# Weight sums of the Strassen products: made by accumulating DMA instead of VectorE

## The reference

```python
def swiglu(x, w1, w3, w2):
    return (jax.nn.silu(x @ w1) * (x @ w3)) @ w2

h1 = LN1(ALPHA * x + 0.5 * swiglu_1(x))
h2 = LN2(ALPHA * h1 + Mixer(h1))         # pooling, windowed attention, gates
y  = LN3(ALPHA * h2 + 0.5 * swiglu_2(h2))
```

## Time and profile before

| | us |
|---|---|
| median of 3 runs (lowest, highest) | 1071.97 (1071.76, 1073.37) |
| span of the profiled execution | 1069.7 |
| PE busy | 1041.3 |
| DVE busy | 806.8 |
| ACT busy | 480.6 |
| POOL busy | 115.7 |

### The profile page before, as it was taken

How to read it: one execution, slowest core, us unless ns; L and a number is a source line. 1 busy time by engine, 2 the same in 40 slices (tenths; PEclk the granted TensorE clock), 3 DMA queues, 4 the chain that set the end, 5 groups by cost and what they waited for, 6 DMA issues and landing times.

```text
span 1069.7 us, 20766 instructions
## 1 busy us (share of the span) xinstructions
PE 1041.3 (97%) x8177; PEld 1024.2 (96%) x8177; DVE 806.8 (75%) x1310; ACT 480.6 (45%) x849; POOL 115.7 (11%) x123
## 2 busy tenths in 40 slices
PE   8999999999999989999999999989999999999995
PEld 8999999999999979998899999979999999999995
DVE  6994999548996775987555576899589973899766
ACT  5543555215554343474542252645355531455424
POOL 2000000000002455000000015400000000000054
PEclk9999999999999999999999999999999999999998
DMA  9332422323234132211132251112332332223302
GB/s 330 105 104 94 145 100 99 109 71 114 84 108 150 59 121 84 84 61 30 51 100 78 96 182 40 40 46 94 110 108 86 114 119 79 80 99 100 119 1 84
DMA packets 60064, 103.70 MB, mean 97 GB/s; under 512 B 6648, under 2 KB 19256, under 8 KB 59944
## 3 DMA queue, kind: packets, MB, share of 16 engines
q1 hardware_dynamic: 58656, 97.94, 27.5%
q0 software_dynamic: 1312, 4.44, 1.2%
HBM read 99.86 MB, written 3.68 MB: 97 GB/s over the span
## 4 chain that ended last, share of the span: by engine, by line
PE 87%; DVE 6%; issue 3%; ACT 2%; POOL 1%; DMA 1%; SPq 0%; DVEq 0%; POOLq 0%; ACTq 0%
PE psum L1631 15%; PE psum L1633 15%; PE psum L1632 15%; PE psum L1705 13%; PE psum L1706 13%; PE psum L1707 13%; DVE stat L1285 1%; PE psum L1841 1%; DVE act_lo L1306 1%; PE psum L1857 1%; DMA xin<-in_x 1%; DVE y L1296 1%; PE psum L1874 0%; ACT y L831 0%; DVE y L1274 0%
## 5 line engine op out<-in xcount | busy, mean ns | idle before, releaser
L1705 PE MATMUL psum<-t_op,ring_hi 128*128 128x272 f32 x640 | 184.1, 288 | 5.2 <-DVE ring_lo L1095 2.7
L1707 PE MATMUL psum<-t_op,ring_lo 128*128 128x272 f32 x640 | 184.8, 289 | 0.0
L1706 PE MATMUL psum<-t_op,ring_hi 128*128 128x272 f32 x640 | 184.1, 288 | 0.0
L1088 DVE TENSOR_TENSOR ring_lo<-raw,ring_hi 128x1024 fp32r<-128x1024 f32 (+2 forms) x87 | 97.1, 1116 | 99.6 <-ACT ring_hi L773 99.2
L1631 PE MATMUL psum<-act_hi,ring_hi 128*128 128x272 f32 x512 | 150.4, 294 | 7.3 <-DVE act_lo L1306 3.2
L1633 PE MATMUL psum<-act_hi,ring_lo 128*128 128x272 f32 x512 | 148.5, 290 | 0.0
L1632 PE MATMUL psum<-act_lo,ring_hi 128*128 128x272 f32 x512 | 148.1, 289 | 0.0
L1631 PE MATMUL psum<-hid,ring_hi 128*128 128x272 f32 x512 | 147.4, 288 | 0.0
L1632 PE MATMUL psum<-hid,ring_hi 128*128 128x272 f32 x512 | 147.0, 287 | 0.0
L1633 PE MATMUL psum<-hid,ring_lo 128*128 128x272 f32 x512 | 146.8, 287 | 0.0
L793 ACT ACTIVATE ring_hi<-sums 128x512 fp32r<-128x512 f32 x160 | 99.7, 629 | 102.6 <-PE psum L1707 66.9
(11 more groups left out here) (250 smaller groups left out, 2448.8 us busy)
## 6 DMA issues: line engine op xcount, KB each, us to landing
raw<-in_ffn_up SPq DMA_DIRECT2D x175, 256.0 KB, 2.9
raw<-in_ffn_down SPq DMA_DIRECT2D x64, 256.0 KB, 2.9
raw<-in_mix_wide SPq DMA_DIRECT2D x52, 256.0 KB, 2.9
raw<-in_ffn_down SPq DMA_DIRECT2D x32, 192.0 KB, 2.5
raw<-in_mix_proj SPq DMA_DIRECT2D x32, 128.0 KB, 2.2
raw<-in_w_out SPq DMA_DIRECT2D x16, 256.0 KB, 2.8
y<-in_x SPq DMA_DIRECT2D x2, 1088.0 KB, 12.6
xin<-in_x SPq DMA_DIRECT2D x3, 544.0 KB, 7.0
```

The source lines that it names most:

```text
L1088: dve.tensor_tensor(lo[:, 0:kn, :], raw[:, n % RAWS, 0:kn, :], hi[:, 0:kn, :], ALU.subtract) \
L1705: pe.matmul(o, w[0][:, k, :], x[0], start=k == 0, stop=False)
L1706: pe.matmul(o, w[0][:, k, :], x[1], start=False, stop=False)
L1707: ins = pe.matmul(o, w[1][:, k, :], x[0], start=False, stop=k == HK - 1)
```

## The change

DVE's `weight_sum` and its places in the order go. POOL issues the sums as DMAs from device memory, in a new function `quarter_sums`: for each pair a plain DMA of the first term of each of the four sums, and then DMAs that add a further term to what is in the slot, each of 256 KB and each behind a wait until the one before it in the same slot has landed. The sums 5, 6, 7 and 3 have 2, 3, 2 and 4 terms, 11 DMAs for a pair. A second tile `sums_odd` holds the slots of odd pairs, so a slot is written again when DVE has split the same sum of the pair but one before. The DMAs only add, so the sums are taken with plus signs alone (a21 + a22; that and a11; a11 + a21; all four), and the signs in the activations' terms and in the combination of product 4 are changed to match. SP loads only the second half (a22) of a pair's second block, and the first block's slot waits for the splits of products 1 and 2 alone. POOL's calls: pairs 0 to 11 of the first mixing directly behind the constants, ahead of the stores of line 680; pairs 12 to 19 ahead of the first norm sums; all 20 of the second mixing behind `center_rest(1)`, from the moment that PE has done the output projection. The area in which POOL's DMA descriptors are kept is set to 4096 bytes, which makes room for `sums_odd`.

```diff
-        sum_done = sem("sum_done")
+        sum_dma = {name: [sem(f"s{k}_dma{i}") for i in range(2)] for name, k in ((5, 1), (6, 2), (7, 3), (3, 4))}
...
+        def sum_slot(q, name):
+
+            return (sums_odd if q % 2 else sums)[:, {5: 0, 6: 1, 7: 2, 3: 3}[name]]
+
+        def sum_landed(engine, li, p, name):
+
+            q = PAIRS * li + p
+            engine.wait_ge(sum_dma[name][q % 2], 16 * TERMS[name] * (q // 2 + 1))
...
+        TERMS = {5: 2, 6: 3, 7: 2, 3: 4}
...
                 if h == 0:
-                    sp.wait_ge(sum_done, 4 * (PAIRS * li + pair + 1))
+                    sp.wait_ge(op_lo, PRODS * li + POS[pair, 1] + 1)
                 sp.wait_ge(op_lo, PRODS * li + POS[pair, 4 if h else 2] + 1)
...
-                        if down:
+                        if item[0] == "pair" and item[3] == 1:
+                            for k0 in (HK, HK + HK // 2):
+                                part = slice(k0 * P, (k0 + HK // 2) * P)
+                                sp.dma_start(flat[:, n % RAWS:n % RAWS + 1, part], up[:, n_up:n_up + 1, part]) \
+                                    .then_inc(raw_in[n % RAWS], 16)
+                        elif down:
...
+            def quarter_sums(li, lo, hi):
+
+                up = a[f"ffn{li + 1}_up"].rearrange("u p k n -> p u k n")
+                for p in range(lo, hi):
+                    q, f0 = PAIRS * li + p, PLAIN + 2 * p
+                    a11 = up[:, f0, 0:HK]
+                    a21, a22 = up[:, f0 + 1, 0:HK], up[:, f0 + 1, HK:KD]
+                    if li and p == 0:
+
+                        for c in range(2):
+                            pool.wait_ge(mm_done[c], FFN2_BASE)
+                    a12 = up[:, f0, HK:KD]
+                    parts = {5: (a21, a22), 6: (a21, a22, a11), 7: (a11, a21), 3: (a12, a11, a21, a22)}
+                    for k in range(4):
+                        for name in (5, 6, 7, 3):
+                            if k >= TERMS[name]:
+                                continue
+                            landed, done = sum_dma[name][q % 2], 16 * (TERMS[name] * (q // 2) + k)
+                            if k == 0:
+                                if q > 1:
+                                    pool.wait_ge(op_lo, PRODS * ((q - 2) // PAIRS) + POS[(q - 2) % PAIRS, name] + 1)
+                                pool.dma_start(sum_slot(q, name), parts[name][k]).then_inc(landed, 16)
+                            else:
+                                pool.wait_ge(landed, done)
+                                pool.dma_start(sum_slot(q, name), parts[name][k], accum_op=ALU.add).then_inc(landed, 16)
+
+            quarter_sums(0, 0, FIRST_PAIR[2])
...
+            quarter_sums(0, FIRST_PAIR[2], PAIRS)
             all_norm_sums(0)
...
             center_rest(1)
+            quarter_sums(1, 0, PAIRS)
             all_norm_sums(2)
...
-                    act.wait_ge(sum_done, 4 * (PAIRS * li + p) + {5: 1, 6: 2, 7: 3, 3: 4}[name])
+                    sum_landed(act, li, p, name)
...
-                first, second = ((part(0, 1), part(0, 0)), (part(1, 1), terms[0]), (part(1, 1), part(0, 1)),
-                                 (part(1, 0), terms[1]))[i]
-                dve.tensor_tensor(terms[i], first, second, ALU.subtract).then_inc(term_sum, 1)
+                if i in (1, 3):
+                    ins = dve.scalar_tensor_tensor(out=terms[i], in0=terms[i // 2], scalar=-1.0,
+                                                   in1=part(1, 1 if i == 1 else 0), op0=ALU.mult, op1=ALU.subtract)
+                else:
+                    first, second = ((part(0, 0), part(0, 1)), None, (part(1, 1), part(0, 1)))[i]
+                    ins = dve.tensor_tensor(terms[i], first, second, ALU.subtract)
+                ins.then_inc(term_sum, 1)
...
-                    dve.tensor_tensor(held[:, e + 2:e + 4, :], psum[:, 3:5, 0:C], spread(u3), ALU.add) \
+                    dve.scalar_tensor_tensor(out=held[:, e + 2:e + 4, :], in0=psum[:, 3:5, 0:C], scalar=-1.0,
+                                             in1=spread(u3), op0=ALU.mult, op1=ALU.subtract) \
                         .then_inc(combined, 1)
...
-    nc = bacc.Bacc("TRN2", target_bir_lowering=False, num_devices=1)
+    nc = bacc.Bacc("TRN2", target_bir_lowering=False, num_devices=1, dynamic_dma_scratch_size=4096)
```

More of the change, by code:

```diff
@@ L167 @@
               {("U", 0, 1): 0, ("U", 1, 1): 1, ("U", 2, 1): 2, ("U", 3, 1): 3})
[L168 to L185, removed]
 def splits_after(li, step):
@@ L300, in program @@
         raw = sb("raw", [P, RAWS, KD, P])
+        sums_odd = sb("sums_odd", [P, 4, HK, P])
         band = sb("band", [P, 2 * WIN])
@@ L523, in op_source @@
                 return raw[:, f1 % RAWS, HK:KD, :]
-            return sums[:, {5: 0, 6: 1, 7: 2, 3: 3}[name]]
+            return sum_slot(PAIRS * li + p, name)
+        def sum_slot(q, name):
[3 more added lines that the diff above has]
+            engine.wait_ge(sum_dma[name][q % 2], 16 * TERMS[name] * (q // 2 + 1))
         def term_home(i, low):
@@ L1095, in split_op @@
                 dve.tensor_tensor(lo, op_source(li, i), hi, ALU.subtract).then_inc(op_lo, 1)
[L1097 to L1120, removed]
             def term(li, i):
@@ L1369, in ffn @@
                     before = step
-                    for i in sums_at(li, step) if kind == "P" else ():
-                        weight_sum(li, i)
                     if kind == "U":
@@ L1400, in ffn @@
                             last_down(l, o, c)
-                    for i in sums_at(li, step) if kind != "P" else ():
-                        weight_sum(li, i)
                     if waiting:
```

## The result

The changed kernel took **1401.9 us** (median of 4 runs, 1397.7 to 1411.2) against 1072.1 for the kernel before beside it: 1.309 times as long, with an interval of 1.306 to 1.312. The forecast was 1234 with a range of 1085 to 1400. So the direction was that of forecast (A), and its mechanism in the main; the loss, 330 us, is twice the 162 us that were forecast, 168 us more.

What follows compares the result with a forecast made beforehand. PE, busy 97%, was taken as the bound, with POOL's DMA chain stalling it after the change: 1071.97 + 120 (four groups of eight) + 29 (first group) + 13 (second mixing) = 1234 us, range 1085 to 1400.

Steps and rivals of the forecast that it cites:

- (A): Sums' DMAs on POOL: transfers queue and an addition doubles engine time; 1234 us, chance 0.50 with the clock as upper part.
- What bounds the kernel, and the gain: PE, busy 97%, bounds it; relieving DVE pays only at the second mixing's start, where PE waits for it.
- cap of 5.5: Start of second mixing: two PE gaps and a slow stretch shrink or close, at most 5.5 us, the whole possible gain.
- The mechanism: POOL's chain of dependent transfers delays sum 3; ACT's queued copies, then DVE and PE wait, PE for ring_lo, growing through groups.
- X: Time of one pair's DMAs on POOL, set by sum 3's four successive transfers: 17.4 us against 10.54 that PE uses.
- The engine time of an addition: DMA engines: an accumulating 256 KB DMA also reads its slot, so 1.56 us against 0.78 for a plain one.
- rival (C): Transfers of a round do not queue, the chain keeps pace with PE: X 10.8 us, kernel 1068 us; chance 0.13.
- From X to the time: Product groups: each of eight 30 us more, first group 29, second mixing's first 13; about 28 us per us of X.
- The rest, 14 us: Outside the product groups: POOL's other duties moved little; smaller descriptor area set at nothing, at most a few us.
- The clock (E): PE's matmuls in late pairs all at 1.2 GHz: 51 us on top of (A), 1285 us; small part expected.
- The signs to look for: For (A): ring_lo waits growing through a group, DMA share near 0.9, additions landing in 4 to 5 us.
- (D): Accumulating or its issue dearer: rounds of 7.7 us, X 25 us, 1484 us; landings over 6 us; chance 0.15.

Runs made afterwards that it cites:

- experiment 2: Changed kernel with the seven accumulating DMAs of each pair left out, only the four plain first terms kept: 1065.6 us, ratio 0.994 to the kernel before.
- experiment 1: Changed kernel with each of a pair's seven accumulating DMAs made a plain copy, same waits and issues: 1216.7 us, ratio 1.1345.
- experiment 5: Layer's computation left out; POOL alone issues plain and accumulating DMAs, singly and in bursts: 3.4 us a plain link, 4.24 us an adding one.
- experiment 6: Computation left out; POOL issues six pairs' DMAs per phase: with raw loads 16.4 us a pair plain, 21.4 adding, 18.1 adding in another order.
- experiment 7: The isolated pair pattern of experiment 6 with the descriptor area at default size instead of 4096 bytes: 586 us for 582 in all.
- experiment 3: Changed kernel with two terms a sum, third and fourth terms left out (four plain, four accumulating DMAs a pair): 1075.1 us, ratio 1.003.
- experiment 10: Kernel before, order alone changed: VectorE makes two early sums of the second mixing's pair 1 later, no sums by DMA: 1071.5 us, ratio 1.0.

## Why the prediction missed: point by point

- **What bounds the kernel, and the gain.** Right. What is taken from DVE brings 6.4 us (experiment 2), at the one place where PE waited for it. The forecast's cap of 5.5 was 0.9 short of the medians, and 0.3 short of the stretch itself.
- **The mechanism.** Right in the main: POOL's chain of dependent additions sets X, and PE stalls late in a group. The path from the landing to PE was wrong in three links. PE waits not for ring_lo (5.3 us in all) but for the combination (line 1184) that frees its psum bank. That combination is not held up by ACT's copies, which were ready 11.9 us or more before; it stands behind a low part in DVE's queue. And the landing that ends each of the 26 stalls is that of sum 6's third term; sum 3's fourth sets the end of a group and, through POOL's queue, the start of the next pair. The waits do not grow through a group: they are 7 to 12 us in each late pair. These links move a stall within its pair; the sum of the prediction used only X, the landing of sum 3 and the work behind it.
- **The engine time of an addition**, a = 1.56 us from the 512 KB row kctxT. Right: 1.62 us in experiment 1, 1.53 and 1.7 in experiment 5. With it, rival (C) could have been given less than 0.13, by a floor that the prediction did not work out: 7 x 1.56 + 4 x 0.78 + 2.3 = 16.3 us of the engines for each pair, above 10.5 whatever the latency.
- **X, 17.4 us. This is the step that failed.** Against the average of the nine pairs of the changed kernel, from a pair's first issue:

| us | forecast | measured |
|---|---|---|
| first addition is issued | 3.0 | 5.8 |
| third term of sum 3 is issued | 13.0 | 17.7 |
| fourth term of sum 3 is issued | 16.9 | 22.0 |
| next pair | 17.4 | 22.85 |

Half of the 5.45 us is lost before the first addition. The sum was made for one pair from a quiet start; but the pair before has just issued its own fourth term, and that is ahead of the new pair's first ones (3.86 against some 5.4 us in experiment 6). The other half is spread over the links: alone, a plain one takes 3.4 us from start to start where the forecast had 2.9, and an addition is issued in 0.86 in place of 0.54 us, seven times a pair. In the isolated patterns: plain with raw loads 16.4 for 13.3 forecast (3.1 us of the miss, with no addition in it); adding on top 5.0 us for 4.1 (0.9); and 1.45 us that only the layer adds. Of these some 0.6 are the slow settling of the isolated phase (22.0 in its last three steps); the cause of the other 0.85 stays open, but it is not the slots, for which none of the nine pairs waits.
- **The Trainium skill** (DMA: Bandwidth & Descriptors, Anatomy of one DMA) gives, by its fit, an estimate of 2.6 us for a plain link of 256 KB; the runs show 3.1 to the landing and 3.4 to the next start even alone, and a median landing of 6.4 for the plain ones in the kernel. What the Trainium skill says of all issuing engines (DMA: Bandwidth & Descriptors, Issuing engines are not separate DMA queues), that their transfers interleave on the same 16 DMA engines, agrees with the trace: SP's own 256 KB loads went from 2.9 to 5.3 us.
- **From X to the time.** Right. The third pair's sum 3 lands 25 us after a group of eight begins (24.9 to 25.7; forecast 20). With that and X = 22.85 the prediction's own sum gives T + 25 + 5 x 22.85 + 7.3 = T + 146.5 (measured 141.8 to 145.3). The last pair of the first group starts at 92.5 and its sum 3 lands 25.7 later, which gives 92.5 + 25.7 + 7.3 = 125.5 (124.9). Its rate of 28 us for each us of X gives 1234 + 28 x 5.45 = 1387, 315 us above the kernel before, and the six product groups of the table have 315 us more.
- **The rest, 14 us, was set at nothing.** The four down stages take 10.3 us more; in the one from 307.4 PE waits 1.8 us for hid, once, and its clock is 0.97 where it was 1.00. The smaller descriptor area, of which the prediction allowed a few us, shows no cost in the kernel's order (experiment 7).
- **The clock (E).** PEclk fell to 0.80 and 0.82 in the groups shown, and PE's matmuls took 12.2 us longer in the first of them, but the time does not show it: a stall ends with a landing, so what the matmuls take, the stall loses. POOL's chain has the same X with PE idle altogether, less 1.45, and behind a group's last landing, where a slow PE would tell, the six groups end after 5.0 to 6.7 us, where the forecast had 7.3.
- **The signs to look for.** Of the two signs of (D) one came: an issue well above 0.54 us (0.86). The other, accumulating DMAs that land in over 6 us, did not: their median is 5.3, just above the 4 to 5 of (A); the 6.0 to 6.2 of the page are medians over first terms (6.4) and additions together. The DMA share came out lower than it said, 0.8 for 0.9. With an X of 22.85 the truth lies between (A), 17.4, and (D), 25, nearer to (D), though the price that (D) was built on, a whole round of 7.7 us, did not occur.
- **The range.** It ended at X = 23.3 on the prediction's formula; X was inside it. What pushed the time past 1400 was the 14 us beside the chain.

## What to carry to other kernels

A chain of dependent DMAs is priced from start to start, in its steady state and with its predecessor still in flight, not by the median landing of independent ones: 3.4 us, plain and alone, became 5.8 to the first addition, and 4.35 from an addition of sum 3 to the next. An accumulating DMA of 256 KB takes the DMA engines twice as long as a copy, so four-term sums at this rate are too dear for the engines before latency is even asked about: add up the engine time of the unit of work first. Where an engine is in the way at one place only, relieve it there: one pair of forty by DMA gave 3.4 us, all forty cost 330.

## What the runs showed of the hardware that I had not expected

- Issuing an accumulating DMA holds POOL for 0.86 us at each size tried (64, 256 and 512 KB), a plain one for 0.54 (256 and 512 KB).
- An accumulating DMA has 64 packets more than the 80 of a plain one of 256 KB and 1.5 to 1.7 us of engine time for 0.78, while the MB counted stay the same.
- A quarter of the size does not make a quarter of the time: 64, 256 and 512 KB land after 2.7, 3.9 and 5.3 us when adding; 256 and 512 KB after 3.1 and 3.4 us when copying.
- DMA engines that are 98% busy, with transfers that take 7 us, cost PE nothing as long as each comes before its use (experiment 3).
- A gap of PE that was closed gave no time back where the granted clock then stood lower: 0.79 for 0.89 over 16 us (experiment 10, one trace).
